# Expert dots that read their normalised rows from PSUM, with scores in two banks

## The reference, cut to what matters

```
x = x + mixed @ w_out
xn = rms_norm(x, norm2_g)
q = (xn @ wq).reshape(c, 8, 2, 128)
s1, s2 = einsum('chd,kd->chk', q[:, :, 0], k1), einsum(... q[:, :, 1], k2)
v1, i1 = top_k(s1, 16); v2, i2 = top_k(s2, 16)
sc, ci = top_k(v1[..., :, None] + v2[..., None, :], 16)
expert = i1[ci // 16] * 128 + i2[ci % 16];   gate = softmax(sc)
a = einsum('chkd,cd->chk', u_tab[expert], xn)          # the dots
y = x + einsum('chk,chkd->cd', gate * gelu(a), v_tab[expert])
```

## Time and profile before

| | |
|---|---|
| three runs | 1870.47, 1873.16, 1877.69 us (median 1873.16) |
| the profiled execution | 1872.7 us, its span 1870.9 us |
| PE | busy 1479.4 us, 79% of the span |
| DVE | 1055.4 us, 56% |
| ACT | 373.1 us, 20% |
| POOL | 1212.5 us, 65% |
| moved by DMA | 618.34 MB, 331 GB/s over the span |

### The profile page before, as it was taken

One profiled execution on the slowest core, in us unless ns is written; L12 is line 12 of the kernel. 1 busy time (PEld: TensorE's weight loads), 2 busy tenths in 40 slices (PEclk: granted clock), 3 DMA queues, 4 the chain that ended last, 5 costly groups with the idle time before them and its releaser, 6 DMA issues.

```text
span 1870.9 us, 14659 instructions
## 1 busy us (share of the span) xinstructions
PE 1479.4 (79%) x4385; PEld 628.6 (34%) x4385; DVE 1055.4 (56%) x2681; ACT 373.1 (20%) x891; POOL 1212.5 (65%) x1291
## 2 busy tenths in 40 slices
PE   8974887879599677768986677799777777777789
PEld 4553563423144222223432222244222222222233
DVE  4945414866948954445698444448954445444430
ACT  2233231022122111111221111112221111111111
POOL 0007500587776777777677777777777777777763
PEclk9987689899799999999998999999899999999999
DMA  8026071789998999999989999999999999999996
GB/s 325 30 70 165 27 304 50 261 309 338 355 345 328 345 365 409 382 372 411 407 325 337 369 408 408 408 410 347 352 360 410 409 410 410 409 410 409 409 394 229
DMA packets 171054, 618.34 MB, mean 331 GB/s; under 512 B 19728, under 2 KB 25184, under 8 KB 169984
## 3 DMA queue, kind: packets, MB, share of 16 engines
q0 software_dynamic: 156928, 571.18, 79.7%
q1 hardware_dynamic: 14048, 46.22, 7.3%
HBM read 610.52 MB, written 5.19 MB: 329 GB/s over the span
## 4 chain that ended last, share of the span: by engine, by line
POOL 25%; PE 19%; DVE 16%; DMA 14%; issue 9%; ACT 1%; DVEq 0%
PE sb_peer_acc L1546 15%; POOL sb_peer_U L1186 14%; DMA sb_kept_V<-peer_v,sb_kept_expert 13%; POOL sb_kept_V L1195 12%; DVE sb_peer_U L1352 4%; PE sb_peer_pq L1471 3%; DVE sb_peer_hot L1287 1%; DVE sb_peer_f L1290 1%; DVE sb_peer_idx L1239 1%; DVE sb_peer_idx L1231 1%; DVE sb_peer_left L1232 1%; DMA sb_peer_U<-peer_u,sb_kept_expert 1%; DVE sb_peer_val L1236 1%; DVE sb_peer_hot L1289 1%; DMA sb_peer_U<-peer_u,sb_peer_es 1%
## 5 line engine op out<-in xcount | busy, mean ns | idle before, releaser
L1546 PE MATMUL sb_peer_acc<-sb_kept_V,sb_peer_dg 128*128 128x512 f32 (+1 forms) x2176 | 1049.5, 617 | 308.1 <-DMA sb_kept_V<-peer_v,sb_kept_expert 212.6
L1352 DVE CUSTOM_DVE_ANT_0 sb_peer_U<-sb_peer_U,sb_rows_xn 128x1024 f32<-128x1024 f32 x512 | 619.8, 1224 | 545.6 <-DMA sb_peer_U<-peer_u,sb_kept_expert 538.7
L1546 PEld LDWEIGHTS sb_peer_acc<-sb_kept_V,sb_peer_dg 128*128 128x128 f32 (+1 forms) x2176 | 379.1, 188 | 954.4 <-issue 500.1
L1186 POOL DMA_INDIRECT sb_peer_U<-peer_u,sb_kept_expert x512 | 531.1, 1037 | 184.4 <-issue 151.1
L1195 POOL DMA_INDIRECT sb_kept_V<-peer_v,sb_kept_expert x512 | 538.8, 1052 | 170.1 <-issue 105.4
L1428 ACT ACTIVATE sb_peer_dg<-sb_kept_ident,sb_peer_wt 128x128 f32<-128x128 f32 (+1 forms) x544 | 210.8, 395 | 1064.7 <-PE sb_peer_acc L1546 832.6
L1186 POOL DMA_INDIRECT sb_peer_U<-peer_u,sb_peer_es x32 | 39.8, 1243 | 127.0 <-DVE sb_peer_es L1291 105.5
L1471 PE MATMUL sb_peer_pq<-sb_rows_wq,sb_peer_xnT 128*128 128x512 f32 x256 | 115.5, 605 | 1.1 <-ACT sb_peer_xnT L1380 1.1
L626 POOL MEMSET sb_rows_wq<- 16x4096 f32 x1 | 3.5, 3506 | 117.1 <-POOLq L161 117.1
L463 PE MATMUL sb_proj_pz<-sb_proj_w_in,sb_proj_xT 128*128 128x512 f32 (+1 forms) x192 | 72.4, 539 | 7.9 <-DVE sb_proj_xT L292 7.9
L1471 PEld LDWEIGHTS sb_peer_pq<-sb_rows_wq,sb_peer_xnT 128*128 128x128 f32 x256 | 49.5, 194 | 64.7 <-issue 63.1
(11 more groups left out here) (259 smaller groups left out, 989.7 us busy)
## 6 DMA issues: line engine op xcount, KB each, us to landing
sb_peer_U<-peer_u,sb_kept_expert POOLq DMA_INDIRECT x512, 6.6
sb_kept_V<-peer_v,sb_kept_expert POOLq DMA_INDIRECT x512, 6.6
sb_proj_w_in<-w_in SPq DMA_DIRECT2D x8, 640.0 KB, 10.8
sb_kept_V<-w_out SPq DMA_DIRECT2D x1, 4096.0 KB, 15.4
sb_proj_xT<-xT SPq DMA_DIRECT2D x8, 272.0 KB, 9.7
sb_proj_x<-x_tok SPq DMA_DIRECT2D x4, 512.0 KB, 12.4
sb_proj_w_mem<-w_mem SPq DMA_DIRECT2D x1, 2048.0 KB, 19.7
sb_blend_MT<-sb_rows_wq SPq DMA_DIRECT2D x8, 256.0 KB, 10.0
```

Of the source, the lines that this page charges most:

```text
L1186: pool.indirect_dma_start(U[:, n % RU, :], None, d["peer_u"], bass.IndirectOffsetOnAxis(ap=rows(n), axis=0)).then_inc(s_u[n % RU], 16)
L1352: dve.tensor_tensor_reduce(U[:, n % RU, :], U[:, n % RU, :], x, 1.0, 0.0, ALU.mult, ALU.add, a[:, g % 2, n % GRP:n % GRP + 1]).then_inc(s_ ...
L1546: mm = pe.matmul(acc[:r, c, :], dg[:, n % RD, 0:r], V[:, n % RV, c * 512:(c + 1) * 512], start=(s == 0), stop=(s == count[k] - 1))
```

## The change

A PSUM tile `xps` of two banks holds the normalised rows of the tile whose dots are running. ACT copies them there in `rows_to_psum`, for the sample tile ahead of `norm(1)`, for the others ahead of the first diagonal of a group, behind the last dot of the tile before. Every dot reads its second operand from `xps`; the first dot of a tile waits for the copy. To make room `psc` shrinks from four banks to two: parts b and b+2 share one, and a part's scores wait until the part two before has been read. Projection 3 writes all of `psc` and waits for the scores of part (1,0) to be read; projection 4 writes `acc` and waits for residual 2, which reads projection 2 from there. PE's loop over the steps waits for residual 4 where it waited for residual 2.

```diff
-        psc = S.ps("psc", [P, 4, 512])
+        psc = S.ps("psc", [P, 2, 512])
+        xps = S.ps("xps", [P, D])
...
-        out_banks = [acc[:, :, :], acc[:, :, :], acc[:, :, :], psc[:, 2:4, :], psc[:, 0:2, :]]
+        out_banks = [acc[:, :, :], acc[:, :, :], acc[:, :, :], psc[:, :, :], acc[:, :, :]]
...
-                    sc = [psc[:r, b, m * P:(m + 1) * P] for m in range(4)]
+                    sc = [psc[:r, b % 2, m * P:(m + 1) * P] for m in range(4)]
...
-                dve.wait_ge(s_xs, 64)
...
-                    x = K.xn[:, order[k], :] if k else xs[:, :]
-                    dve.tensor_tensor_reduce(U[:, n % RU, :], U[:, n % RU, :], x, 1.0, 0.0, ALU.mult, ALU.add,
+                    if n == first[k]:
+                        dve.wait_ge(s_xp, k + 1)
+                    dve.tensor_tensor_reduce(U[:, n % RU, :], U[:, n % RU, :], xps[:, :], 1.0, 0.0, ALU.mult, ALU.add,
                                              a[:, g % 2, n % GRP:n % GRP + 1]).then_inc(s_dot, 1)
...
+                def rows_to_psum(k):
+
+                    if k:
+                        act.wait_ge(s_dot, first[k])
+                        act.wait_ge(s_xn, k + 1)
+                    else:
+                        act.wait_ge(s_xs, 64)
+                    act.activation(xps[:, :], K.xn[:, order[k], :] if k else xs[:, :], ACT.Copy).then_inc(s_xp, 1)
...
+                rows_to_psum(0)
                 norm(1)
...
+                    if n + LAG - 2 in first[1:NT]:
+                        rows_to_psum(first.index(n + LAG - 2))
                     if n % GRP == 0:
...
+                    if k == 3:
+                        pe.wait_ge(s_sr, part(1, 0) + 1)
                     if k == 4:
-                        pe.wait_ge(s_sr, part(1, 0) + 1)
+                        pe.wait_ge(s_h, 3)
...
-                    if k == 1:
-                        pe.wait_ge(s_h, NT if b == 1 else NT - 1 if b else 1)
-                    else:
-                        pe.wait_ge(s_sr, part(k - 1, b) + 1)
+                    if (k, b) == (1, 1):
+                        pe.wait_ge(s_h, NT - 1)
+                    pe.wait_ge(s_sr, part(k, b) - 1 if b or k > 1 else 1)
...
-                pe.wait_ge(s_h, 3)
+                pe.wait_ge(s_h, NT)
```

More of the change, by code:

```diff
@@ L1113, in experts @@
         s_xs = S.sem("sample_rows_spread")
+        s_xp = S.sem("rows_in_psum")
         s_xt = S.sem("rows_turned")
@@ L1501, in scores @@
                     pe.wait_ge(s_qe, part(k, b) + 1)
-                    if k == 1:
-                        pe.wait_ge(s_h, NT if b == 1 else NT - 1 if b else 1)
-                    else:
-                        pe.wait_ge(s_sr, part(k - 1, b) + 1)
+                    if (k, b) == (1, 1):
+                        pe.wait_ge(s_h, NT - 1)
+                    pe.wait_ge(s_sr, part(k, b) - 1 if b or k > 1 else 1)
                     for m in range(4):
                         hh = b * 4 + m
-                        mm = pe.matmul(psc[:r, b, m * P:(m + 1) * P], qT[:, hh, 0:r], keys[:, hh % 2, :], start=True, stop=True)
+                        mm = pe.matmul(psc[:r, b % 2, m * P:(m + 1) * P], qT[:, hh, 0:r], keys[:, hh % 2, :], start=True, stop=True)
                     mm.then_inc(s_sc, 1)
```

## The result

The changed kernel takes 1844.76 us (median of four runs, 1842.07 to 1845.72), the one before 1873.9 us in the same comparison (four runs): a ratio of 0.9842, interval 0.982 to 0.9864, 29 us less. The profiled execution has a span of 1843.2 us, 27.7 less than before. Its time lies 4 us above the forecast of 1841 and inside its range.

A forecast was written before the change was run, and what follows sets the result against it. In quiet stretches the DMA was taken as the limit, elsewhere POOL issues held up by dots. Terms -30 (held-up issues) + 0 - 2 (start) = -32 us gave 1840.7, with 0.5 us 1841 us; range 1815 to 1861.

The forecast's parts named there:

- The mechanism: Dots of the expert phase: a POOL issue starting during a dot with both inputs in SBUF waits until it ends.
- The issues no longer held up: Three stretches after groups of routings, dots 119-215, 247-343, 375-543: -30 us, range -23 to -31.
- the pitch (29.7) over the bytes (22.8): Two ways to size the gain in those stretches: 2.56 us a pair, or the shortage against 409.6 GB/s.
- The rate as the DMA's limit: Quiet stretches: DMA at 409 GB/s sets 2.56 us a pair, so freeing POOL there gives nothing.
- The first rival: Quiet stretches: the DMA takes more once POOL is faster, 2.50 us a pair, 22 us less, 1819 us; chance 0.12.
- Within the groups: Groups of routings, such as 444 to 659 us: DVE is busy and rows have landed; 0, with -4 to +2.
- The start, order on PE: First expert step at 407.6 us, 8.9 us later, just hidden by dot 48; start net -2 us, ends -5 and +4.
- A wait of over 3 us on ACT at 440 to 520 us: Sign of a wrong forecast: DVE idle more than 3 us on PE or ACT between 440 and 520 us.
- The copy at step 32: Dot 32 waits for a copy, a table load and a short gelu, some 2.6 us that were hidden before.
- Scores in two banks: A part's scores wait for the reading of the part two before: taken as 0, up to +3 us.
- tail: Behind the last dot: nothing is changed, it only moves.
- The slow dot out of PSUM: Rival: dots slower from PSUM; 0.21 us more each loses the gain, half rate gives some 2005 us; chance 0.07.

The follow-up runs named there:

- the third experiment: The changed kernel with projection 4 moved to the PSUM tile of the normalised rows and dots 0 to 31 reading from SBUF: 1843.03 us, ratio 0.9851.

## Why the prediction was right

**The mechanism.** The step "an issue that starts during a dot waits until it is over, and only with both inputs in SBUF" is shown from both sides: by undoing the operand alone, and by moving the product instead. One reading under it was off, to no effect: the dot of 1500.91 runs 1.23 us, to 1502.14, and 1502.06 is where the read of its sum starts. The v issue so ends 0.81 us after the dot, the same as the 0.82 us of the earlier trace rows.

**The sum.** -30 + 0 - 2 became -24.2 + 0.6 - 4.0 = -27.7 us, by the spans. That the total is only 4 us off is in part luck: the stretches gave less than forecast and the start more. The low end of the terms adds up to -40 us and not to -41.

**The issues no longer held up, -30 us.** Measured -24.2. The direction held, the size was off: of the two ways to work it out I took the pitch (29.7) over the bytes (22.8), "because a dot needs its own row and not the bytes". With the queue never empty the bytes decide, and some belong to others. Ahead of dot 326 (1204.18) the result of a tile is stored (SP and DVE rows):

```profile
1197.70 0.33 SPq L1171 DMA_DIRECT2D out_y_p<-sb_kept_x  x1
...
1200.43 1.22 DVE L1354 CUSTOM_DVE_ANT_0 sb_peer_U<-sb_peer_U,sb_peer_xps 128x1024 f32<-128x1024 f32 x1 [1.33 <-DMA sb_peer_U<-peer_u,sb_kept_expert]
1204.18 1.22 DVE L1354 CUSTOM_DVE_ANT_0 sb_peer_U<-sb_peer_U,sb_peer_xps 128x1024 f32<-128x1024 f32 x1 [2.52 <-DMA sb_peer_U<-peer_u,sb_kept_expert]
```

The store is 512 KB, and the row behind it comes 1.2 us late. Such a gap of 3.8 us stands ahead of dots 198, 326 and 454, two dots behind a tile's result, one in each stretch and before the change as well, and no faster POOL removes it. The three make 3.6 of the 5.6 us by which the stretches still exceed 2.56 us a pair; the 30 us counted them as POOL's.

**The rate as the DMA's limit, 0 in the quiet stretches.** Right: the three stretches run at 408 to 409 GB/s though POOL issues faster, the landings climb, and with fewer bytes the pitch falls to 2.50 us. The first rival is out. The 425 GB/s that the prediction takes from the Trainium skill ("DMA: Bandwidth & Descriptors", section "Bandwidth") stand there for transfers issued from GpSimd, not for gathers of rows; the gathers here did not reach it.

**Within the groups, 0.** Dots 215 to 247 take 97.7 us after 97.2, 343 to 375 97.2 after 97.1: together 0.6 us more.

**The start, order on PE, -2 us in all.** From dot 0 to dot 119 it came to -3.2 us, and dot 0 itself starts 0.9 us earlier. The first expert step came at 407.62, as forecast (407.6), but by two errors that cancel. Residual 4 was 1.8 us early (397.59 instead of 399.40). And the queries behind it were 1.8 us slower: PE, idle for 4.90 and 5.31 us at its two new waits, came back slower both times (rows of PE and DVE, then the windows of the stretches between the waits, two of them with their first part by itself):

```profile
377.32 16.23 PE L1511 MATMUL sb_peer_acc<-sb_kept_V,sb_rows_xn 128*128 128x512 f32 x32 [4.90 <-DVE sb_kept_x L1211]
397.59 1.21 DVE L1211 TENSOR_TENSOR sb_kept_x<-sb_kept_x,sb_peer_acc 128x1024 f32<-128x1024 f32 x1
398.86 8.83 PE L1485 MATMUL sb_peer_pq<-sb_rows_wq,sb_peer_xnT 128*128 128x512 f32 x16 [5.31 <-DVE sb_kept_x L1211]
```

```profile
358.50:372.40 13.90, 13.90 (x33) 5.89 (x31) 13.45 (x31) 0.03 (x1) 5.27 (x6) 1.00 0.35 104
377.30:393.40 16.10, 16.08 (x32) 6.84 (x32) 10.87 (x17) 4.96 (x8) 2.45 (x3) 0.86 0.53 194
377.30:382.20 4.90, 4.88 (x6) 2.09 (x7) 2.08 (x3) 2.72 (x4) 0.55 (x1) 0.54 1.00 410
398.90:407.60 8.70, 8.70 (x16) 3.53 (x16) 5.94 (x10) 2.66 (x4) 6.87 (x7) 0.80 0.97 357
398.90:402.30 3.40, 3.40 (x4) 1.44 (x5) 0.64 (x2) 2.66 (x4) 2.77 (x3) 0.50 0.95 310
```

The same 32 matmuls took 13.90 us for projection 3 at a mean granted clock of 1.00 and 16.23 us for projection 4 at 0.86, of which the first 4.9 us had 0.54, so nearly all of them 1.2 GHz. The queries took 8.83 us where they took 7.03, the first 3.4 of them at 1.2 GHz. In the third experiment, where PE has neither wait, both took their old time:

```profile
370.76 13.90 PE L1511 MATMUL sb_peer_xps<-sb_kept_V,sb_rows_xn 128*128 128x512 f32 x32
384.49 7.03 PE L1487 MATMUL sb_peer_pq<-sb_rows_wq,sb_peer_xnT 128*128 128x512 f32 x16
```

That cost was missing from the sum. Only the queries' part stands on the way to the first expert step, since they waited for residual 4 and not for projection 4. Dot 48 came at 440.17, held by the gelu as forecast:

```profile
440.17 1.22 DVE L1354 CUSTOM_DVE_ANT_0 sb_peer_U<-sb_peer_U,sb_peer_xps 128x1024 f32<-128x1024 f32 x1 [5.75 <-ACT sb_peer_ga L1437]
```

How the delay was absorbed shows in DVE's waits from 324 to 660 us. Those of dots for their rows fell from 38.2 + 5.0 = 43.2 us to 28.3 + 1.3 = 29.6 us, those of dots and routings for a gelu rose from 6.9 + 3.7 = 10.6 us to 17.0 + 6.7 = 23.7 us: one took the place of the other. A wait of over 3 us on ACT at 440 to 520 us was named as a sign of being wrong; this one, of 5.75 us, ends at its edge, and the next, of 8.68 us ahead of dot 80, was 6.91 us before.

**The copy at step 32** held dot 32 up for 2.62 us, as forecast (2.6); at step 288 the dots stand 2.66 us apart (2.6). **Scores in two banks** and the **tail** cost nothing that shows: 61.7 us from the last dot to PE's end in both.

The slow dot out of PSUM is out (1.219 us on average, 1.224 before).

## What to carry to other kernels

Where GpSimd issues gathers and VectorE runs long elementwise work beside it, look for VectorE instructions with both inputs in SBUF: here an issue that fell into one waited for its end. Move one input to PSUM, and count what that is worth only up to the next limit, here the bytes of the DMA, stores included. Then look again at what had been arranged around the old limit: spreading the routings and cutting them into pieces was worth some 15 us with the operand in SBUF and 57 us with it in PSUM.

## What the runs showed that was not expected

How the other work is cut counts beside how it is spaced: whole routings 24 dots apart gained 9 us over the changed kernel, the same ones in three pieces 57. What the pieces alone would gain, with the old spacing, was not run. And after some 5 us without work PE's granted clock was 0.80 to 0.86 in the next stretch, which made two short waits cost another 4 us of PE time, 1.8 us of it ahead of the first expert step.
